# Splitting two neighbouring weight slabs with one instruction on each engine in a float32 two-layer trunk

## The chip, the cores and the metric

One Trainium2 chip, of which the kernel uses one core. The metric is the device time of one execution in microseconds (us); for the kernel before it is the median of three runs. The engines are TensorE (PE; its weight loads are listed as PEld), VectorE (DVE), ScalarE (ACT), GpSimd (POOL) and SyncE (SP). SP here only issues transfers.

## The reference, cut to what matters

The sequence has 256 tokens of width 2048, all in float32. Layer 0 mixes tokens with windowed attention, layer 1 with a gated block; each layer ends with an MLP of width 8192.

```python
for i in range(2):
    a = rms_norm(h, g[0])
    a = attention(a, w_qkv, w_o) if i == 0 else sgu_mixer(a, w_in, w_s, w_out)
    h = h + rms_norm(a, g[1])
    c = square(relu(rms_norm(h, g[2]) @ w_up[i])) @ w_down[i]
    h = h + rms_norm(c, g[3])
```

`sgu_mixer` takes `z = gelu(h @ w_in)`, splits it into u and v, normalises v over its width (mean and variance), mixes it over tokens with `w_s`, multiplies by u and projects with `w_out`.

## The kernel before, in words

**Products.** Every matrix product is made in three passes of TensorE: each float32 operand is split into a part `hi` that is rounded to the fp32r format and a rest `lo = raw - hi`, and hi*hi, hi*lo and lo*hi are summed (L396, L397, L398). The work is cut into 85 blocks. A block gives 256 tokens x 512 output columns from 2048 input rows, in 96 products of 128x512. Its weights come as eight slabs; a slab has two 128-row parts of 512 columns, 128x1024 in the on-chip memory, 512 KB. Slabs 2p and 2p+1 are pair p; PE takes pair by pair, and in each pair first token half 0 (both slabs), then token half 1. When the second half of a slab is done it counts `slab_used` up.

**Order of the blocks.** 0 is k and v, 1 to 4 are q, 5 to 8 the attention's output, 9 to 40 the first MLP, 41 to 44 the v half and 45 to 48 the u half of the gated block, 49 to 52 its output, 53 to 84 the second MLP. An MLP has four quarters of eight blocks: four up blocks, then four down blocks that add to y. The first quarter begins with `first_block`, in which the input is transposed while PE multiplies; the others begin with a plain block.

**A slab's way.** SP's `load_block` (L293 to L301) puts slab i into raw slot i mod 4 of `w_raw`; before it, it waits on `lo_made` until the slab four before has been subtracted. ACT's `split_slab` (L679 to L684) waits for the landing and until the slot i mod 8 of `w_hi` and `w_lo` is free (`slab_used`), and writes `w_hi`, rounded. DVE's `split_slab` (L1064 to L1067) waits for `hi_made`, writes `w_lo = w_raw - w_hi` and counts `lo_made` up by one, which gives the raw slot back to SP and the slab to PE. Both engines work three pairs (six slabs) ahead of PE: `slab_ahead(blk, i)` names slab i+6.

**Order on the engines.** It is written out by hand. `split_ahead(blk, pair)` calls `split_next` for the two slabs of a pair; `split_next` and the turns below take single slabs. In block 0 and in the attention's `attend` all slabs are single; around them, during the first q block (1), the calls on DVE are single slab 7 of block 0, pair 0, two small copies of v, pairs 1 and 2, single slab 6, the rotation of q (`rotate_q`, L1343 to L1348), and on ACT pairs 0 and 1, then a copy and a single slab twice. PE's next step, the transposes of q (L504), needs the rotation.

**Turns.** The result of up block j must be transposed to be the left operand of a down block. On ACT, the bank is drained (L811), then squared (L846); on DVE, `turn` (L1102 to L1109) makes four groups of four 32x32 transposes (L1098), each group followed by one single slab split; then ACT copies the result to `b_hi` (L710), DVE makes `b_lo` (L1114), and then both engines split pairs 2 and 3. Turn j runs on DVE during block j+1 of the quarter, the last in the first down block, whose pair 3 needs its `b_lo` (`first_down`). The order on ACT in such a block is pairs 0 and 1, `b_hi`, pairs 2 and 3, the drain of the block. In down blocks both engines split four pairs, then DVE adds the sum to y (L1201). In the second block of the first quarter both run behind `first_block`.

**The v half.** DVE takes statistics of each v block (L1491), averages them (L1516, L1519), and after one pair normalises (L1529, L1533) while PE is in block 45; PE's gate products (L653) come at four places in that block and wait for them.

Of the kernel before, what the change touches and what calls it, by code (L numbers as in the profile page):

```python
# [8 lines left out]
F32 = mybir.dt.float32  # L9
F32R = mybir.dt.float32r  # L10
I32 = mybir.dt.int32
ALU = mybir.AluOpType
ACT = mybir.ActivationFunctionType
# [11 lines left out]
RAW_SLOTS = 4  # L25
SLOTS = 8
LEAD = 3
PAIRS = KB // SLAB_KB // 2
# [24 lines left out]
BLOCKS = B_MLP1 + 2 * NB * QUARTERS  # L53
# [36 lines left out]
def trunk(nc, x, positions, gains, w_qkv, w_o, sinks, w_in, ln_g, ln_b, w_s, b_s, w_out, w_up, w_down, out):  # L90
    ctx = ExitStack()
    with ctx:
        def sb(name, shape, dt=F32):
            return ctx.enter_context(nc.sbuf_tensor(name, shape, dt))
# [4 lines left out]
        def sem(name):  # L99
            return ctx.enter_context(nc.semaphore(name))  # L100
# [8 lines left out]
        w_raw = sb("w_raw", [P, RAW_SLOTS, SLAB])  # L109
        w_hi = sb("w_hi", [P, SLOTS, SLAB], F32R)  # L110
        w_lo = sb("w_lo", [P, SLOTS, SLAB], F32R)
# [82 lines left out]
        slab_landed = [sem(f"slab_landed{i}") for i in range(RAW_SLOTS)]  # L194
# [5 lines left out]
        hi_made = sem("hi_made")  # L200
        lo_made = sem("lo_made")
        slab_used = sem("slab_used")
# [49 lines left out]
        def at_least(eng, sem_, value):  # L252

            if not isinstance(value, int) or value > 0:
                eng.wait_ge(sem_, value)
# [24 lines left out]
        def slab_ahead(blk, i):  # L280

            i = i + 2 * LEAD
            return (blk, i) if i < 2 * PAIRS else (blk + 1, i - 2 * PAIRS)
# [394 lines left out]
        def _(act):  # L678
            def split_slab(blk, i):  # L679

                act.wait_ge(slab_landed[i % RAW_SLOTS],
                            blk * (32 * PAIRS // RAW_SLOTS) + 16 * (i // RAW_SLOTS + 1))
                at_least(act, slab_used, blk * (2 * PAIRS) + (i + 1 - SLOTS))
                nc.scalar.activation(w_hi[:, i % SLOTS, :], w_raw[:, i % RAW_SLOTS, :], ACT.Copy).then_inc(hi_made, 1)  # L684
# [5 lines left out]
            def split_next(blk, *slabs):  # L690
                for i in slabs:
                    if not (isinstance(blk, int) and blk == BLOCKS - 1 and i + 2 * LEAD >= 2 * PAIRS):
                        split_slab(*slab_ahead(blk, i))

            def split_ahead(blk, pair):
                split_next(blk, 2 * pair, 2 * pair + 1)

            def split_unit(n, use0, norm, units=UNIT):

# [72 lines left out]
            def first_block(blk, use0, norm, evac):  # L772
# [9 lines left out]

                split_unit(2, use0, norm)
                split_ahead(blk - 1, 3)
                split_unit(3, use0, norm)
                split_unit(4, use0, norm)
# [12 lines left out]
                act.wait_ge(norm_done, norms[0])  # L799
                evac(0)  # L800
                split_ahead(blk, 2)
                evac(1)
                split_ahead(blk, 3)

            h_seen = [0]
# [253 lines left out]
        def _(dve):  # L1059
# [4 lines left out]
            def split_slab(blk, i):  # L1064

                dve.wait_ge(hi_made, blk * (2 * PAIRS) + (i + 1))
                nc.vector.tensor_tensor(w_lo[:, i % SLOTS, :], w_raw[:, i % RAW_SLOTS, :],  # L1067
                                        w_hi[:, i % SLOTS, :].bitcast(F32), ALU.subtract).then_inc(lo_made, 1)
# [5 lines left out]
            def split_next(blk, *slabs):  # L1074
                for i in slabs:
                    if not (isinstance(blk, int) and blk == BLOCKS - 1 and i + 2 * LEAD >= 2 * PAIRS):
                        split_slab(*slab_ahead(blk, i))

            def split_ahead(blk, pair):
                split_next(blk, 2 * pair, 2 * pair + 1)  # L1080

            def split_unit(n, use0, norm, units=UNIT):
                pair, t = units[n]
# [87 lines left out]
            def first_block(blk, use0, norm):  # L1171

                split_unit(2, use0, norm)
                split_ahead(blk - 1, 3)
                update_h(4)
                split_unit(3, use0, norm)
                update_h(5)
                split_unit(4, use0, norm)
                update_h(6)
                split_next(blk, 0)  # L1180
                split_unit(5, use0, norm)
                split_next(blk, 1)
                update_h(7)
                split_unit(6, use0, norm)
                split_next(blk, 2)
                split_unit(7, use0, norm)
                sums[0] += 2 * TOK
                dve.wait_ge(norm_sum, sums[0])
                link(nc.vector.tensor_tensor(sum_sq[:, :], pre_ssq[:, 0, :], pre_ssq[:, 1, :], ALU.add))
                mean()  # L1190
                inverse(r_in)
                split_next(blk, 3)
                split_ahead(blk, 2)
                split_ahead(blk, 3)
# [401 lines left out]
```

## Time and profile before

| what | value |
|---|---|
| median of three runs | 1921.07 us (1920.85 to 1921.43) |
| span of the profiled execution | 1919.6 us |
| PE busy | 1909.2 us, 99%, 8604 products and transposes |
| DVE busy | 1340.6 us, 70% |
| ACT busy | 959.1 us, 50% |
| bytes read from HBM | 365.52 MB, 192 GB/s over the span |
| granted clock of TensorE, mean | 0.999 |

The profiled execution's span goes from its first to its last instruction; what lies around it is in the run's time and not in the span, and the median of the runs is 1.5 us above this span. Times in rows are in us from the span's start; "mean ns" is the duration of one instruction. Two instructions one behind the other on ACT or DVE overlap by about 0.1 us, so that two of 1.06 take 2.0 together.

### The profile page before, as it was taken

To read this page: it belongs to the slowest core of one execution; us is meant where nothing else is said; L and a number is where in the kernel's file an instruction comes from. 1 tells how busy PE (TensorE), PEld (TensorE's weight loads), DVE (VectorE), ACT (ScalarE), POOL (GpSimd) and SP (SyncE) were. 2 spreads that over 40 slices of the span, in tenths; PEclk is the share of its full clock that TensorE was granted. 3 is DMA by queue.
4 is the path that set the end of the run, shared out by engine and by line. 5 is a ranking of instruction groups with operands and counts; after the bars stand their busy time and mean duration, and the time that the engine had idled before them with its cause. 6 is when DMAs were issued, how large, how long until landed. Compare 5 with 4: busy or idle time off the path is not lost.

```text
span 1919.6 us, 25731 instructions
## 1 busy us (share of the span) xinstructions
PE 1909.2 (99%) x8604; PEld 1572.2 (82%) x8604; DVE 1340.6 (70%) x1872; ACT 959.1 (50%) x1294; POOL 6.2 (0%) x23
## 2 busy tenths in 40 slices
PE   9999999999999999999999999999999999999998
PEld 7777888888888888888888888888888888888886
DVE  6886588657755865686768885787568557846864
ACT  7766475435534543544554454645354445434542
POOL 0000000000000000000000000000000000000000
PEclk9999999999999999999999999999999999999999
DMA  7546566655665565556485656566556655665663
GB/s 248 179 134 209 175 198 196 216 191 178 200 201 175 189 214 187 186 187 233 142 262 178 191 189 208 170 199 217 193 178 194 211 190 190 194 199 169 199 202 110
DMA packets 188691, 368.72 MB, mean 192 GB/s; under 512 B 11450, under 2 KB 11588, under 8 KB 187844
## 3 DMA queue, kind: packets, MB, share of 16 engines
q1 hardware_dynamic: 187280, 360.75, 58.2%
q0 software_dynamic: 1040, 6.82, 1.0%
q8 instruction: 51, 0.84, 0.2%
q14 instruction: 28, 0.23, 0.0%
q10 hardware_dynamic: 292, 0.08, 0.0%
HBM read 365.52 MB, written 2.10 MB: 192 GB/s over the span
## 4 chain that ended last, share of the span: by engine, by line
PE 98%; ACT 1%; DVE 1%; DMA 1%; issue 0%; SPq 0%; DVEq 0%; ACTq 0%
PE acc L396 16%; PE acc L398 16%; PE acc L397 16%; PE scores L396 15%; PE scores L398 15%; PE scores L397 15%; PE t L421 1%; PE scores L524 0%; PE o L543 0%; PE o L653 0%; DMA h<-in_x 0%; DMA w_raw<-in_attn_w_qkv 0%; DVE w_lo L1067 0%; PE t L534 0%; ACT L941 0%
## 5 line engine op out<-in xcount | busy, mean ns | idle before, releaser
L1067 DVE TENSOR_TENSOR w_lo<-w_raw,w_hi 128x1024 fp32r<-128x1024 f32 x679 | 818.9, 1223 | 314.7 <-ACT w_hi L684 297.7
L684 ACT ACTIVATE w_hi<-w_raw 128x1024 fp32r<-128x1024 f32 x679 | 703.7, 1057 | 529.9 <-PE scores L398 212.6
L1098 DVE STREAM_TRANSPOSE work<-s 32x256 f32<-32x256 f32 x544 | 237.1, 436 | 100.7 <-ACT s L846 90.8
L396 PE MATMUL acc<-w_hi,a_hi 128*128 128x512 f32 x768 | 303.4, 395 | 0.1
L398 PE MATMUL acc<-w_hi,a_lo 128*128 128x512 f32 x768 | 299.4, 390 | 0.0
L397 PE MATMUL acc<-w_lo,a_hi 128*128 128x512 f32 x768 | 299.0, 389 | 0.0
L396 PE MATMUL scores<-w_hi,a_hi 128*128 128x512 f32 x672 | 262.4, 390 | 0.0
L398 PE MATMUL scores<-w_hi,a_lo 128*128 128x512 f32 x672 | 261.5, 389 | 0.0
L397 PE MATMUL scores<-w_lo,a_hi 128*128 128x512 f32 x672 | 261.5, 389 | 0.0
L396 PE MATMUL acc<-w_hi,b_hi 128*128 128x512 f32 x640 | 249.8, 390 | 0.0
L396 PE MATMUL scores<-w_hi,b_hi 128*128 128x512 f32 x640 | 249.2, 389 | 0.0
L398 PE MATMUL acc<-w_hi,b_lo 128*128 128x512 f32 x640 | 249.1, 389 | 0.0
L397 PE MATMUL acc<-w_lo,b_hi 128*128 128x512 f32 x640 | 249.0, 389 | 0.0
L398 PE MATMUL scores<-w_hi,b_lo 128*128 128x512 f32 x640 | 249.0, 389 | 0.0
L397 PE MATMUL scores<-w_lo,b_hi 128*128 128x512 f32 x640 | 249.0, 389 | 0.0
L396 PEld LDWEIGHTS acc<-w_hi,a_hi 128*128 128x128 f32 x768 | 144.2, 188 | 31.5 <-issue 1.2
L398 PEld LDWEIGHTS acc<-w_hi,a_lo 128*128 128x128 f32 x768 | 144.2, 188 | 30.5
L397 PEld LDWEIGHTS acc<-w_lo,a_hi 128*128 128x128 f32 x768 | 144.3, 188 | 28.9
L396 PEld LDWEIGHTS scores<-w_hi,a_hi 128*128 128x128 f32 x672 | 126.2, 188 | 26.2 <-issue 0.2
L398 PEld LDWEIGHTS scores<-w_hi,a_lo 128*128 128x128 f32 x672 | 126.2, 188 | 26.2
L397 PEld LDWEIGHTS scores<-w_lo,a_hi 128*128 128x128 f32 x672 | 126.2, 188 | 25.9
L710 ACT ACTIVATE b_hi<-work 128x1024 fp32r<-128x1024 f32 x36 | 38.2, 1062 | 207.2 <-DVE work L1098 207.2
(159 smaller groups left out, 1396.6 us busy)
## 6 DMA issues: line engine op xcount, KB each, us to landing
w_raw<-in_mlp_w_up SPq DMA_DIRECT2D x256, 512.0 KB, 3.8
w_raw<-in_mlp_w_down SPq DMA_DIRECT2D x256, 512.0 KB, 4.6
w_raw<-in_sgu_w_in SPq DMA_DIRECT2D x64, 512.0 KB, 4.5
w_raw<-in_attn_w_qkv SPq DMA_DIRECT2D x39, 512.0 KB, 4.6
w_raw<-in_attn_w_o SPq DMA_DIRECT2D x32, 512.0 KB, 4.8
w_raw<-in_sgu_w_out SPq DMA_DIRECT2D x32, 512.0 KB, 4.6
gain<-in_norm_gains POOLq DMA_DIRECT2D x4, 1024.0 KB, 6.4
h<-in_x SPq DMA_DIRECT2D x8, 256.0 KB, 6.1
```

Source lines behind the costliest of these rows:

```text
L396: nc.tensor.matmul(bank[t][:, :], lhsT=x_hi[:, kb, tok], rhs=w1, start=(kb == 0), stop=False)
L397: nc.tensor.matmul(bank[t][:, :], lhsT=x_hi[:, kb, tok], rhs=w2, start=False, stop=False)
L398: last = nc.tensor.matmul(bank[t][:, :], lhsT=x_lo[:, kb, tok], rhs=w1, start=False, stop=(kb == KB - 1))
L421: last = nc.tensor.transpose(tb[n % 2][:, k * P:(k + 1) * P], h[:, t, f:f + P], ident[:, :])
L684: nc.scalar.activation(w_hi[:, i % SLOTS, :], w_raw[:, i % RAW_SLOTS, :], ACT.Copy).then_inc(hi_made, 1)
L710: nc.scalar.activation(b_hi[:, bass.ds(j * 4, 4), :], sT, ACT.Copy).then_inc(b_hi_made, 1)
L1067: nc.vector.tensor_tensor(w_lo[:, i % SLOTS, :], w_raw[:, i % RAW_SLOTS, :], w_hi[:, i % SLOTS, :].bitcast(F32), ALU.subtract).then_inc(lo ...
L1098: last = nc.vector.transpose(turned[:, :, :, src * 32:src * 32 + 32], part[:, :, :, dst * 32:dst * 32 + 32])
```

## The change

A pair that `split_ahead` asks for is now split by one instruction of 128x2048 on each engine, `split_two`. ACT waits for both slabs' landing and for the eight-slot buffer to have room for both, and counts `hi_made` up by two at the end; DVE waits for that, and counts `lo_made` up by two at the end. `split_next` and the four single splits of a turn stay as they were, and so do the loads of SP, each of which waits for its own slot.

```diff
--- before.py
+++ after.py
@@ -692,8 +692,18 @@
                     if not (isinstance(blk, int) and blk == BLOCKS - 1 and i + 2 * LEAD >= 2 * PAIRS):
                         split_slab(*slab_ahead(blk, i))
 
+            def split_two(blk, i):
+
+                for k in (i, i + 1):
+                    act.wait_ge(slab_landed[k % RAW_SLOTS],
+                                blk * (32 * PAIRS // RAW_SLOTS) + 16 * (k // RAW_SLOTS + 1))
+                at_least(act, slab_used, blk * (2 * PAIRS) + (i + 2 - SLOTS))
+                at, raw = i % SLOTS, i % RAW_SLOTS
+                nc.scalar.activation(w_hi[:, at:at + 2, :], w_raw[:, raw:raw + 2, :], ACT.Copy).then_inc(hi_made, 2)
+
             def split_ahead(blk, pair):
-                split_next(blk, 2 * pair, 2 * pair + 1)
+                if not (isinstance(blk, int) and blk == BLOCKS - 1 and 2 * pair + 2 * LEAD >= 2 * PAIRS):
+                    split_two(*slab_ahead(blk, 2 * pair))
 
             def split_unit(n, use0, norm, units=UNIT):
 
@@ -1076,8 +1086,16 @@
                     if not (isinstance(blk, int) and blk == BLOCKS - 1 and i + 2 * LEAD >= 2 * PAIRS):
                         split_slab(*slab_ahead(blk, i))
 
+            def split_two(blk, i):
+
+                dve.wait_ge(hi_made, blk * (2 * PAIRS) + (i + 2))
+                at, raw = i % SLOTS, i % RAW_SLOTS
+                nc.vector.tensor_tensor(w_lo[:, at:at + 2, :], w_raw[:, raw:raw + 2, :],
+                                        w_hi[:, at:at + 2, :].bitcast(F32), ALU.subtract).then_inc(lo_made, 2)
+
             def split_ahead(blk, pair):
-                split_next(blk, 2 * pair, 2 * pair + 1)
+                if not (isinstance(blk, int) and blk == BLOCKS - 1 and 2 * pair + 2 * LEAD >= 2 * PAIRS):
+                    split_two(*slab_ahead(blk, 2 * pair))
 
             def split_unit(n, use0, norm, units=UNIT):
                 pair, t = units[n]
```

## Rows read from the trace of the kernel before

**Rows 1.** the profile page: part 1's PE line and two groups of part 5
```profile
PE 1909.2 (99%) x8604; PEld 1572.2 (82%) x8604; DVE 1340.6 (70%) x1872; ACT 959.1 (50%) x1294; POOL 6.2 (0%) x23
...
L1067 DVE TENSOR_TENSOR w_lo<-w_raw,w_hi 128x1024 fp32r<-128x1024 f32 x679 | 818.9, 1223 | 314.7 <-ACT w_hi L684 297.7
L684 ACT ACTIVATE w_hi<-w_raw 128x1024 fp32r<-128x1024 f32 x679 | 703.7, 1057 | 529.9 <-PE scores L398 212.6
```

**Rows 2.** waits of the load queue: engine, line, releaser, us, times, longest
```profile
SPq L300 <- DVE w_lo L1067: 1415.0, 662, 14.5
```

**Rows 3.** instruction groups by form: the two half slabs of 512 columns
```profile
L1153 DVE TENSOR_TENSOR w_lo<-w_raw,w_hi 128x512 fp32r<-128x512 f32 x1 | 0.7, 686 | 0.0
...
L742 ACT ACTIVATE w_hi<-w_raw 128x512 fp32r<-128x512 f32 x1 | 0.6, 627 | 0.0
```

**Rows 4.** busy us (x count) of PE, PEld, DVE, ACT, POOL; clock, DMA, GB/s
```profile
300.00:322.00 22.00, 22.00 (x99) 18.23 (x98) 19.92 (x29) 11.40 (x13) 0.00 (x0) 1.00 0.66 212
```

**Rows 5.** DVE's timeline, start us and us, last pairs before the first turn
```profile
263.90 2.36 DVE L1067 TENSOR_TENSOR w_lo<-w_raw,w_hi 128x1024 fp32r<-128x1024 f32 x2 [1.50 <-ACT w_hi L684]
267.04 2.36 DVE L1067 TENSOR_TENSOR w_lo<-w_raw,w_hi 128x1024 fp32r<-128x1024 f32 x2 [0.78 <-ACT w_hi L684]
```

**Rows 6.** ACT's timeline in blocks 10 to 12
```profile
265.96 1.99 ACT L684 ACTIVATE w_hi<-w_raw 128x1024 fp32r<-128x1024 f32 x2
268.90 1.06 ACT L684 ACTIVATE w_hi<-w_raw 128x1024 fp32r<-128x1024 f32 x1 [0.95 <-DMA w_raw<-in_mlp_w_up]
270.99 1.06 ACT L684 ACTIVATE w_hi<-w_raw 128x1024 fp32r<-128x1024 f32 x1 [1.03 <-DMA w_raw<-in_mlp_w_up]
...
308.39 1.06 ACT L684 ACTIVATE w_hi<-w_raw 128x1024 fp32r<-128x1024 f32 x1 [1.18 <-DMA w_raw<-in_mlp_w_up]
```

**Rows 7.** DVE's timeline in blocks 11 to 13
```profile
303.30 1.23 DVE L1067 TENSOR_TENSOR w_lo<-w_raw,w_hi 128x1024 fp32r<-128x1024 f32 x1
...
312.08 1.77 DVE L1098 STREAM_TRANSPOSE work<-s 32x256 f32<-32x256 f32 x4 [1.36 <-ACT s L846]
...
331.83 1.78 DVE L1098 STREAM_TRANSPOSE work<-s 32x256 f32<-32x256 f32 x4 [1.25 <-ACT s L846]
...
343.95 1.22 DVE L1114 TENSOR_TENSOR b_lo<-work,b_hi 128x1024 fp32r<-128x1024 f32 x1
```

**Rows 8.** PE's timeline: first product of block 13, first of its fourth pair
```profile
329.31 0.39 PE L396 MATMUL acc<-w_hi,b_hi 128*128 128x512 f32 x1
...
345.63 0.39 PE L396 MATMUL acc<-w_hi,b_hi 128*128 128x512 f32 x1
```

**Rows 9.** start of the first head group: ACT's timeline, then the critical chain
```profile
47.81 1.06 ACT L684 ACTIVATE w_hi<-w_raw 128x1024 fp32r<-128x1024 f32 x1 [2.80 <-DMA w_raw<-in_attn_w_qkv]
...
54.20 1.23 DVE w_lo L1067
...
56.42 0.66 PE t L504 x4
```

**Rows 10.** the quarter of blocks 17 to 24: DVE's timeline, then PE's
```profile
517.21 1.22 DVE L1114 TENSOR_TENSOR b_lo<-work,b_hi 128x1024 fp32r<-128x1024 f32 x1
...
519.71 0.39 PE L396 MATMUL acc<-w_hi,b_hi 128*128 128x512 f32 x1
```

**Rows 11.** value blocks and layer norm: timelines of ACT, DVE and PE
```profile
969.04 1.06 ACT L684 ACTIVATE w_hi<-w_raw 128x1024 fp32r<-128x1024 f32 x1 [1.65 <-DMA w_raw<-in_sgu_w_in]
...
1024.96 1.06 ACT L684 ACTIVATE w_hi<-w_raw 128x1024 fp32r<-128x1024 f32 x1 [0.30 <-PE scores L398]
...
1032.21 0.17 DVE L1519 TENSOR_SCALAR mean_sq<-moments 128x2 f32<-128x2 f32 x1
...
1036.20 1.42 DVE L1533 SCALAR_TENSOR_TENSOR y<-y,r_out,work 128x512 f32<-128x512 f32 x2
...
1038.30 0.38 PE L653 MATMUL o<-y,work 128*128 128x256 f32 x1
```

**Rows 12.** loads issued from 985.0 to 986.6 us: time to landing
```profile
DMA to landing us min/median/max: 7.3/7.3/7.3
```

## The prediction

> **What bounds the kernel now.** I read the page first. TensorE (PE) is busy 1909.2 of 1919.6 us [rows 1], so only about 10 us are idle, nearly all before the first product. An edit that takes no product away can gain next to nothing in the middle; it can only lose, where it makes PE wait. VectorE (DVE) and ScalarE (ACT) are at 70% and 50%: idle there costs nothing by itself. The same rows show the two instructions that are merged, 679 of each: 1057 ns on ACT, 1223 ns on DVE, DVE waiting mostly for ACT and ACT mostly for PE.
>
> Next the load queue's own waits: SP waits 1415 us for the DVE subtraction that gives a raw slot back [rows 2]. So the loads run as early as the four raw slots allow, and a slot's round trip (given back, loaded, rounded by ACT, subtracted by DVE) is what to watch. Then the timeline where DVE is fullest: it is busy 19.92 of 22 us in the second to fourth block of the first MLP [rows 4]. Nine times (eight quarters and the gated block's output) such a chain of turns ends in a down product, and there I compared DVE's end with PE's need.
>
> **PE's pace.** Block 13 (the first down block of MLP 0) starts at 329.31 and its fourth pair at 345.63 [rows 8]: 5.44 us a pair, 21.76 us a block. Four raw slots are one turn of 10.88 us.
>
> **Costs of the parts.** *ACT:* 128x512 takes 626 ns, 128x1024 takes 1057 [rows 1, 3]: 431 ns per 512 columns, so 128x2048 takes about 1.91 us, against 1.99 for two back to back. Ends 1.91 (slope) and 2.1 (two full ones); I take 1.91. *DVE:* 686 and 1223 ns [rows 1, 3] give 2.30 us, against 2.36 for two [rows 5]; ends 2.30 and 2.45. So merging saves some 0.1 us of engine time a pair, in idle engines, worth nothing to PE. *The new waits:* ACT waits for both landings and for the second slab's split slots (PE ends it six products, 1.36 us, after the first slab's); DVE waits for both w_hi; both raw slots come free at the end of 2.30 us. Behind ACT's wait stand its drains of PE's banks, behind DVE's the transposes, the rotation and the norm.
>
> *One slot's trip:* a subtraction ends at 303.30+1.23=304.53 and ACT starts on the slab loaded into that slot at 308.39 [rows 6, 7]: 3.9 us with the issue. *Two slots at once:* no row shows it. The nearest: two slots given back 1.14 us apart, at 265.12 and 266.26 (the two end at 263.90+2.36 [rows 5], the first 1.14 sooner), and ACT starts on their successors at 268.90 and 270.99 [rows 6]. The second came 4.7 us after its own slot, 5.9 after the first's. So a pair takes between 4.7 and 5.9; I take 5.3, the middle, because the two transfers clearly share something and start now together.
>
> The Trainium skill, "SBUF — State Buffer", The DMA setup-cost knee, fits a DMA as about 2 us plus bytes at 436 GB/s; by it a pair of 1 MiB would be 4.4 us, an estimate from that page, and the sum below would be near 11 us instead of 18.
>
> Plain blocks: 5.3+1.91+2.30+0.1=9.6 us against 10.88. They keep pace; a merged slab is ready 16.32-1.91-2.30=12.1 us ahead of PE, a single one 14.0. Cost zero, covered by the three pairs of lead. What follows are the four places with no such cover.
>
> **1. First query block, about +2.9 us.** Here PE waits already: its transposes at 56.42 come after DVE's rotation of q (L1343 to L1348), which stands behind the single subtraction of 54.20 to 55.43 [rows 9], that behind ACT's rounding, and that behind a load into the first slot of what is now a merged pair. That pair's second slab reaches ACT only at 47.81 [rows 9]. Merged: ACT 47.8 to 49.7, DVE to 52.05, both slots back; +3.9 gives ACT 55.95 to 57.0, DVE to 58.25. The rotation starts 58.25-55.43 = 2.8 us later, and so does PE, with small change 2.85. Ends 2.7 and 3.9 (load 3.7 to 4.9).
>
> **2. and 3. First quarter of each MLP, +6.1 us each.** The turn in DVE is four groups of transposes (1.78) and four single subtractions (1.23), 12.1 us. After it the last slot's load (3.9), ACT's rounding, ACT's drain of the finished block (from 308.39+1.06=309.45 to the next transposes at 312.08: 2.63 [rows 6, 7]) and the next turn. Before: 12.1+3.9+1.06+2.63=19.7, as 312.08 to 331.83 is [rows 7]. That is 2 us a block less than PE, so DVE catches up, and its last b_lo ends at 343.95+1.22=345.17 for a need at 345.63: 0.5 us of room.
> After, by steps. The pair before the first turn ends its subtraction at about 270.6 instead of 267.04+2.36=269.40 [rows 5] (ACT can start between 265.96 [rows 6] and 266.9, where its second single one did; the middle). First transposes at 270.6. The first single subtraction of the turn waits for a merged w_hi: slots back at 267.0, +5.3, +1.91 = 274.2, 1.85 us of wait. Turn over at 284.65; +3.9+1.91 = 290.45; drains 2.6, b_hi 1.05, b_lo 1.22: second turn at 295.4. Its successor: 12.1+3.9+1.91+2.6 = 20.5, at 315.9; the next again with 1.05 of wait for the merged w_hi, at 337.45. b_lo of the fourth turn ends 1.0+12.1+1.22 later, 351.8. PE needs it at 345.63: +6.1. DVE no longer catches up, because the period is 21.6. At 4.7 for a pair it is 4.3, at 5.9 it is 7.9. The second MLP has the same order and offsets; I count it alike.
> The other six quarters, and the chain before block 49, begin from a plain block: there the last b_lo ends at 517.21+1.22=518.43 for a need at 519.71 [rows 10], and the turns start when PE ends, not behind the loads: by the same steps they stay 0.1 to 0.3 late, under 1.28. Cost zero; gone, if a pair takes over 6.5.
>
> **4. Value blocks and layer norm, +3.0 us.** The first merged pair starts on ACT at 969.04 with its load late [rows 11]; DVE done 973.3. Six trips of 9.6 and about 1.5 of contention with the gate weights' load (two slabs issued there took 7.3 us to land [rows 12], some 1.5 over a pair's 5.9) end at 1032.4; at PE's pace they would end at 1029.2 (ACT free to start at 1024.96 [rows 11], +1.91+2.30), in time for the statistics. Then transposes 0.9, statistics 1.4, means 0.4: mean_sq at 1035.2 instead of 1032.21. The normalised half ends at 1036.20+1.42 and PE's gate wants it at 1038.30 [rows 11]: 0.7 of room, so PE waits 2.3; the fourth gate, behind two more merged subtractions, 0.7 more. Ends 0.9 (pair 4.7) and 6.
>
> **Sum.** 2.85+6.1+6.1+3.0 = 18.0 us on a profiled 1919.6 us span; the median of the runs, 1921.07, is 1.5 above the span, and I add to it: **1939.1 us**. Ends: 2.7+8.6+0.9=12.2, and 3.9+15.8+6=25.7.
>
> **Rivals.**
> *A, the forecast* (waits at four places), chance 0.70.
> *B, loads of a pair land nearly together,* ACT served after 4.2 us. For: issues will be 0.4 us apart, not 1.14. Against: 268.90 and 270.99, 2.1 apart. By the same steps a quarter costs 2.9, the norm 0.5, place 1 the same: 1921.07+9.2=1930.3, a little less if more than that is covered. Chance 0.12.
> *C, not slower:* with fewer loads in flight each is served sooner, in place 2 above all, where the last slot's load stands in every turn. The point from which it decides is 3.0 us for one load (in place of 3.9) and 3.8 for two: then each quarter loses 0.8, place 1 2.0, the norm nothing, 3.6 in all: 1924.7, and 1922 if it is faster still. For: between two pairs the queue is now empty for longer. Against: in a turn slots come back 3.05 us apart, so those loads were nearly alone already and took the 3.9. Chance 0.08.
> *D, all blocks:* if a pair's trip passes 6.6 us, the round exceeds 10.88 everywhere; at 7.0 it is 0.8 us a block, some 50 us over about 70 blocks less the lead: about 1960. For: two loads took 7.3 us beside another [rows 12]. Against: that was one place, and the round has 1.3 us to spare. Chance 0.08.
> *E, faster:* in 300 to 322 DVE is nearly full [rows 4]; two merged subtractions save 0.12 a block, 0.5 in a quarter. That gives 1920.6, with the short wait before 56.42 gone. It is faster by over 0.2% only if much else shifts. Chance 0.02.
> The Trainium skill, "Perfetto Trace Analysis", Optimizing Scalar/DVE Operations, says both: grouping helps a saturated engine (E), and where the engine is not saturated but causes bubbles elsewhere, breaking instructions up may finish work sooner. By the second this change is the wrong way round; with DVE at 70% of the span the trace bears out the second.
>
> **Range and chances.** Ends of A are 1933 and 1947; downwards I take in most of B: 1928 to 1947, leaving out C, D and E. A measurement of this kernel tells about 0.2%, 3.8 us. Faster 0.02, same 0.08 (C), slower 0.90 (A, B, D).
>
> **What would show it.** In the changed trace: subtractions of 2.30 and roundings of 1.91; slabs of a pair reaching ACT 5.3 after the subtraction; the first q transposes near 59.3; a PE gap of about 6 us at the fourth pair of blocks 13 and 57 with b_lo as its end, none in the other six; a gap of about 2 us at the first gate. PE's other steps 0.227 us as before. Wrong would be: PE busy share still 99% of a span under 1924, or waits for w_lo in the plain blocks (D).

## The result, and the profile after

The changed kernel takes 1954.91 us (median of five runs, 1953.37 to 1957.82) against 1921.09 (1920.85 to 1921.43, five runs): a ratio of 1.0179, 95% interval 1.0168 to 1.0189. It is slower, as forecast, but by 33.8 us and not by 18.0, and the time lies outside the range of 1928 to 1947. The profiled execution has a span of 1951.6 us, the shortest of its five (the others 1952.6 to 1956.0), and 1.8 us lie around it; before it was 1919.6. The 32.0 us between these two spans are what is accounted for below.

The page of the changed kernel, to be read beside [rows 1]:

```profile
PE 1916.3 (98%) x8604; PEld 1576.3 (81%) x8604; DVE 1317.0 (67%) x1634; ACT 911.1 (47%) x985; POOL 6.2 (0%) x23
...
L702 ACT ACTIVATE w_hi<-w_raw 128x2048 fp32r<-128x2048 f32 x309 | 591.6, 1915 | 695.2 <-DMA w_raw<-in_mlp_w_down 210.3
L1093 DVE TENSOR_TENSOR w_lo<-w_raw,w_hi 128x2048 fp32r<-128x2048 f32 x238 | 545.6, 2292 | 488.2 <-ACT w_hi L702 486.7
```

The instructions last what was forecast: 1.915 us on ACT, 2.292 on DVE. Both engines work less, ACT by 48 us and DVE by 24. PE executes the same 8604 instructions and is nevertheless busy for 7.1 us longer: besides waiting, it ran slower somewhere, which the table below finds. Next, PE's waits in the changed kernel (what waited, the releaser: us in total, times, longest):

```profile
PE acc L396 <- DVE b_lo L1132: 15.7, 2, 8.2
PE t L504 <- DVE s L1366: 2.8, 1, 2.8
PE acc L396 <- DVE w_lo L1093: 2.8, 3, 0.9
PE o L653 <- DVE y L1551: 2.4, 1, 2.4
...
PE o L653 <- DVE y L1559: 1.0, 1, 1.0
```

Four of these lines belong to the four forecast places: the last `b_lo` of the two first quarters (one line), the rotated q, and the two lines of the norm. The `w_lo` line was not forecast.

To divide the 32.0 us, the start of each product was compared with the start of the same product before; each row is a step in the difference.

| where | step, us | forecast |
|---|---|---|
| the start of the kernel | -0.8 | 0 |
| q transposes before block 2 | +2.7 | 2.85 |
| the next products of block 2 | +1.5 | 0 |
| blocks 9, 41, 53, fifth slab | +1.2 each, 3.5 in all | 0 |
| block 13, fourth pair | +8.3 | 6.1 |
| the rest of block 13 | +2.4 | 0 |
| block 45, gate; block 46 | +2.65 and +1.2 | 2.3 and 0.7 |
| block 49 | +0.3 | 0 |
| block 57, fourth pair | +7.7 | 6.1 |
| the rest of block 57 | +2.5 | 0 |

The third, sixth and last rows are places where PE waits for nothing and still falls behind. The windows of the changed kernel behind the wait in block 13 show why (columns as in [rows 4]; the clock stands before the DMA share):

```profile
350.00:358.00 8.00, 0.36 (x2) 0.00 (x0) 7.42 (x12) 3.81 (x3) 0.00 (x0) 0.69 0.51 166
358.00:362.00 4.00, 3.49 (x8) 2.81 (x9) 2.75 (x2) 1.46 (x2) 0.00 (x0) 0.50 0.43 131
362.00:366.00 4.00, 4.00 (x16) 3.18 (x15) 2.50 (x2) 1.40 (x1) 0.00 (x0) 0.84 0.78 255
366.00:370.00 4.00, 4.00 (x20) 3.30 (x19) 1.97 (x3) 1.92 (x1) 0.00 (x0) 1.00 0.74 217
```

PE stands idle from 350.4 to 358.5, and while it stands its granted clock falls from 1.0 to 0.5, from 2.4 to 1.2 GHz. The products after the wait find it there. PE's timeline of the changed kernel, at the same place:

```profile
358.51 0.79 PE L396 MATMUL acc<-w_hi,b_hi 128*128 128x512 f32 x1 [8.15 <-DVE b_lo L1132]
359.10 0.63 PE L397 MATMUL acc<-w_lo,b_hi 128*128 128x512 f32 x1
359.53 0.63 PE L398 MATMUL acc<-w_hi,b_lo 128*128 128x512 f32 x1
359.95 0.63 PE L396 MATMUL acc<-w_hi,b_hi 128*128 128x512 f32 x1
```

The steps are 0.43 us instead of 0.227. The clock is at half from 353.1 to 363.3, from 1342.9 to 1353.1 and from 59.5 to 62.9. In block 2 it fell only at 59.5, 1.2 us after PE had started again at 58.35.

### The profile page after: what moved, and what is told of

It reads as the page before. It is cut to its first block, busy times and chain, and to the rows that moved or that the text cites. A ratio compares the mean times of both kernels' runs of the same rounds, so it can differ in the third digit from the quotient of the medians.

```text
span 1951.6 us, 25457 instructions
## 1 busy us (share of the span) xinstructions
PE 1916.3 (98%) x8604; PEld 1576.3 (81%) x8604; DVE 1317.0 (67%) x1634; ACT 911.1 (47%) x985; POOL 6.2 (0%) x23
## 4 chain that ended last, share of the span: by engine, by line
PE 86%; DVE 6%; ACT 3%; DMA 3%; issue 2%; SPq 0%; ACTq 0%; DVEq 0%
PE acc L396 14%; PE acc L397 14%; PE acc L398 14%; PE scores L396 14%; PE scores L398 14%; PE scores L397 14%; ACT w_hi L702 2%; DVE work L1116 2%; DVE w_lo L1093 2%; DMA w_raw<-in_mlp_w_up 2%; DVE w_lo L1077 1%; DMA w_raw<-in_mlp_w_down 1%; PE t L421 1%; PE scores L524 0%; PE o L543 0%
## 5 line engine op out<-in xcount | busy, mean ns | idle before, releaser
L702 ACT ACTIVATE w_hi<-w_raw 128x2048 fp32r<-128x2048 f32 x309 | 591.6, 1915 | 695.2 <-DMA w_raw<-in_mlp_w_down 210.3
L1093 DVE TENSOR_TENSOR w_lo<-w_raw,w_hi 128x2048 fp32r<-128x2048 f32 x238 | 545.6, 2292 | 488.2 <-ACT w_hi L702 486.7
L1077 DVE TENSOR_TENSOR w_lo<-w_raw,w_hi 128x1024 fp32r<-128x1024 f32 x203 | 247.3, 1224 | 24.4 <-ACT w_hi L702 16.6
L396 PEld LDWEIGHTS acc<-w_hi,b_hi 128*128 128x128 f32 x640 | 121.3, 190 | 43.3 <-DVE b_lo L1132 16.9
```

Source lines behind the costliest of these rows:

```text
L396: nc.tensor.matmul(bank[t][:, :], lhsT=x_hi[:, kb, tok], rhs=w1, start=(kb == 0), stop=False)
L702: nc.scalar.activation(w_hi[:, at:at + 2, :], w_raw[:, raw:raw + 2, :], ACT.Copy).then_inc(hi_made, 2)
L1093: nc.vector.tensor_tensor(w_lo[:, at:at + 2, :], w_raw[:, raw:raw + 2, :], w_hi[:, at:at + 2, :].bitcast(F32), ALU.subtract).then_inc(lo_m ...
```

## The experiments

Each variant is told by its difference from the kernel before or from the changed one. Where only one time is given, one run was timed beside the kernel before (1920.8 to 1921.2 us) and its span and steps are what is compared, with 1919.6. The five spans of the changed kernel lie 4.4 us apart, so where two variants that wait like it differ by less in their totals, only the steps at the places tell something.

### Which engine's half costs what

The first run merges on ACT alone, the second on DVE alone, each with the other engine's `split_ahead` as before:

```diff
 def split_ahead(blk, pair):        # of the engine that stays as before
-    if not (isinstance(blk, int) and blk == BLOCKS - 1 and 2 * pair + 2 * LEAD >= 2 * PAIRS):
-        split_two(*slab_ahead(blk, 2 * pair))
+    split_next(blk, 2 * pair, 2 * pair + 1)
```

> ACT rounds a pair with one instruction, DVE subtracts slab by slab and gives each raw slot back by itself. Theory T (the joint give-back lengthens a raw slot's trip): the waits shrink but stay, since the rounding still waits for both landings and ends 0.9 us later than the second single one: about 0.5 us at the first q transposes, 0.3 at each of the three first blocks, 4 to 6 with some clock loss at each first quarter, 1 to 2 at the norm; the span is 12 to 18 us over the 1919.6 of before. Rival R (DVE's instruction of 128x2048, which cannot start before both w_hi and blocks its engine for 2.3 us, is the cause): with it gone the span is within 3 us of before.

> ACT rounds slab by slab as before, DVE subtracts a pair with one instruction and gives both slots back together. Theory T: about 2 us at the first q transposes, 1.2 at each of the three first blocks (the pair's w_lo is late for PE's fifth slab), 0.6 at block 13 and nothing at block 57, because the turns' period stays at 19.8 us and DVE catches up, 1.5 to 2.5 at the norm; the span is 6 to 10 us over before. Rival R (the DVE instruction is the cause of all): over 20 us.

ACT alone: 1939.98 us, span +18.6, which is 0.6 over its range. DVE alone: 1929.04 us, span +7.6, inside its range, but in part by luck: the norm costs 0.3 us in all where 1.5 to 2.5 were expected, block 13 nothing where 0.6 was, and 1.6 us went behind q at half clock, which was not in the sum. PE's waits with ACT alone merged:

```profile
PE acc L396 <- DVE b_lo L1131: 10.2, 2, 5.5
PE t L504 <- DVE s L1365: 1.7, 1, 1.7
```

And with DVE alone merged:

```profile
PE acc L396 <- DVE w_lo L1092: 3.1, 3, 1.0
PE t L504 <- DVE s L1365: 2.0, 1, 2.0
```

So the two halves hurt at different places. ACT's merge makes the last `b_lo` late in both first quarters; DVE's alone never does, but it makes the three first blocks lose 1.3 us each. Together they cost 32.0, which is 5.8 more than 18.6 and 7.6. By places, the waits of the two first quarters grow from 10.5 us (ACT alone) and nothing (DVE alone) to 16.0, and the gate in block 45, which neither alone delays, loses 2.65; at q and in the first blocks the two together cost less than the sum. In the quarters and at the gate one delay feeds the other.

### The waits without the long instructions

Two more variants of the kernel before, all slabs still split one by one. In the first, DVE counts `lo_made` up by two at a pair's second subtraction, so both slots come back together; in the second, ACT waits for both landings before the first rounding.

```diff
-                split_next(blk, 2 * pair, 2 * pair + 1)
...
+                for half in range(2):
+                    b, i = slab_ahead(blk, 2 * pair + half)
+                    dve.wait_ge(hi_made, b * (2 * PAIRS) + (i + 1))
+                    last = nc.vector.tensor_tensor(w_lo[:, i % SLOTS, :], w_raw[:, i % RAW_SLOTS, :],
+                                                   w_hi[:, i % SLOTS, :].bitcast(F32), ALU.subtract)
+                last.then_inc(lo_made, 2)
```

> The kernel before with one edit on DVE: a pair's two subtractions stay single but count lo_made up only after the second, by two. Theory T: nearly as the kernel in which DVE alone is merged, 5 to 9 us over before, since the slots and the slabs come free at the same times within 0.1 us; if the instruction's size is what costs, under 2 us.

```diff
+                b, i = slab_ahead(blk, 2 * pair)
+                act.wait_ge(slab_landed[(i + 1) % RAW_SLOTS],
+                            b * (32 * PAIRS // RAW_SLOTS) + 16 * ((i + 1) // RAW_SLOTS + 1))
                 split_next(blk, 2 * pair, 2 * pair + 1)
```

> The kernel before with one edit on ACT: before the first of a pair's two roundings it waits for both landings; all instructions are single. Theory T: slots come back 1.1 us apart, so the second lands some 4.7 us after its own and the first rounding waits for it; 0.5 us or less at the q transposes, 0 to 2 at block 13, the norm under 1: the span is 1 to 5 us over before. If the wait alone explains ACT's share, it comes near the kernel in which ACT alone is merged (12 us or more).

The joint give-back alone: 1924.10 us, span +2.7, below what was expected. Of it 0.7 are at the q transposes and 0.8 at each of blocks 9, 41 and 53; nothing at 13 or 57. The joint wait alone: 1925.45 us, span +4.1, as expected, of which 2.3 stand at block 13 and 1.65 at block 57. PE's waits, with the joint give-back and then with the joint wait:

```profile
PE acc L396 <- DVE w_lo L1085: 1.5, 3, 0.5
```

```profile
PE acc L396 <- DVE b_lo L1119: 3.6, 2, 2.1
```

Each is small. Are the long instructions the rest? This run takes the changed kernel and writes each merged instruction as two of 128x1024, while all its waits and counts stay joint:

```diff
-    nc.scalar.activation(w_hi[:, at:at + 2, :], w_raw[:, raw:raw + 2, :], ACT.Copy).then_inc(hi_made, 2)
+    nc.scalar.activation(w_hi[:, at, :], w_raw[:, raw, :], ACT.Copy)
+    nc.scalar.activation(w_hi[:, at + 1, :], w_raw[:, raw + 1, :], ACT.Copy).then_inc(hi_made, 2)
...                                    # likewise for the subtraction on DVE
```

> The changed kernel with each merged instruction written again as two of 128x1024, while every wait and every count stays joint (ACT waits for both landings and both split slots, counts two at the end; DVE waits for both w_hi, gives both slots back at the end). If the loss comes from the joint waits and the joint give-back, the span stays within 3 us of the changed kernel's 1951.6, with the long waits at the fourth pair of blocks 13 and 57. If the long instructions themselves cost it, or if the separate effects simply add (4.1 of waiting for both landings and 2.7 of the joint give-back), the span is 1925 to 1931.

1957.09 us, span 1955.3: 3.7 above the changed kernel's and so 0.7 outside the 3 us, but nowhere near 1931. Most of the 3.7 is the norm, where the step is 5.8 us and 3.4 us at half clock fell. The page of this variant shows the instructions apart again, and its waits the same stall:

```profile
L702 ACT ACTIVATE w_hi<-w_raw 128x1024 fp32r<-128x1024 f32 x309 | 326.9, 1058 | 665.4 <-DMA w_raw<-in_mlp_w_down 203.1
...
L703 ACT ACTIVATE w_hi<-w_raw 128x1024 fp32r<-128x1024 f32 x309 | 322.2, 1043 | 0.0
```

```profile
PE acc L396 <- DVE b_lo L1135: 15.8, 3, 7.9
PE o L653 <- DVE y L1554: 3.9, 1, 3.9
```

The length of the instruction is therefore not the cause. What costs is that a pair is handed on only when it is complete, at three places in a row: landing to ACT, ACT to DVE, DVE to the slots. The handoff from ACT to DVE is in this run and in neither of the two small ones. No run has it alone, so its share is argued and not shown: between the joint wait (+4.1) and ACT merged (+18.6) lie 14.5 us, 4.4 of them at half clock, and what differs is this handoff, ACT's wait for both slabs' room in `w_hi`, and the one instruction.

### Where the loss stands

The changed kernel with single slabs in the first quarter of each MLP alone; its complement, merged pairs there and single slabs elsewhere, has the two values of the flag exchanged:

```diff
             def split_ahead(blk, pair):
+                if one[0]:
+                    split_next(blk, 2 * pair, 2 * pair + 1)
-                if not (isinstance(blk, int) and blk == BLOCKS - 1 and 2 * pair + 2 * LEAD >= 2 * PAIRS):
+                elif not (isinstance(blk, int) and blk == BLOCKS - 1 and 2 * pair + 2 * LEAD >= 2 * PAIRS):
...
+                one[0] = True
                 quarter(0, base, True, False)
+                one[0] = False
```

> The changed kernel with single slabs on both engines in the first quarter of each MLP (blocks 9 to 16 and 53 to 60), pairs elsewhere. If the quarters' waits and the slow clock after them are all of that place's loss: 32.0 less 8.3+2.4 and 7.7+2.5 and two first-block waits of 1.15 leaves about 9 us over before (span near 1928.5). If the pairs cost everywhere and the waits only show it there, it stays over 20 us.

> The kernel before with merged pairs in the first quarter of each MLP alone, the complement of the run with single slabs there. By the places: two waits of about 8 us, two stretches at half clock behind them of 2.4, and the first blocks 9 and 53 at 1.2 each: 23 us, a span near 1942.8. If the 4.5 us that the changed kernel has already lost by then is part of why the quarters are so dear, it is under 1938.

Single there: 1932.00 us (1930.85 to 1935.44, four runs), ratio 1.0060 (1.0045 to 1.0076), span +10.9. That span is 2 us above the 9 expected: PE loses 0.9 us at block 49 and 1.3 on the way into block 53, where the changed kernel lost 0.3 and nothing. Merged there alone: 1943.09 us (1940.84 to 1943.33, four runs), ratio 1.0116 (1.0099 to 1.0133), span +19.5. The two losses add up to 1.76% beside 1.79% for the whole change. PE's waits in the second:

```profile
PE acc L396 <- DVE b_lo L1142: 14.4, 2, 7.5
```

There block 13 waits 7.6 us and block 57 7.1, though PE came to block 13 only 0.6 us late and not 4.6: being late on entry is not what makes the quarters dear. Its span is 3.7 us below the sum that was expected, since the waits are shorter by 1.3 us together and the clock is at half for 6.8 us behind each instead of 10.2.

### The half clock

The changed kernel with 30 extra products on PE, whose result nobody reads, just ahead of the fourth pair of blocks 13 and 57:

```diff
             def first_down(blk, index, idle=0):
                 for pair in range(PAIRS):
+                    if pair == PAIRS - 1:
+                        idle_products(idle)
```

> The changed kernel with 30 extra products into an unused bank (6.8 us at full clock) ahead of the wait at the fourth pair of blocks 13 and 57; their result is never read. Clock theory: TensorE's granted clock fell to 0.5 after the two long waits and cost 2.4 us at each; with PE at work in the wait it stays at 1.0, and the span is 4.5 to 5 us under the changed kernel's 1951.6. Rival (the slow steps are the restart's own, or the products delay the kernel): the same or up to 3 us more.

Windows of this variant, behind the wait and then at the norm:

```profile
358.00:362.00 4.00, 4.00 (x19) 3.28 (x18) 2.29 (x1) 0.89 (x2) 0.00 (x0) 1.00 0.56 132
362.00:366.00 4.00, 4.00 (x20) 3.30 (x19) 2.73 (x2) 1.17 (x1) 0.00 (x0) 1.00 0.71 252
...
1052.00:1060.00 8.00, 5.24 (x17) 4.27 (x18) 7.89 (x11) 1.61 (x1) 0.00 (x0) 0.79 0.51 170
```

The clock stays at 1.00 behind both quarters. The fourth pair starts 7.9 us late in each, as before, and there is no step behind it: the 2.4 and 2.5 us of the table were the clock's. The span is 1949.2, only 2.4 under the changed kernel's where about twice that was expected, because this time 3.4 us at half clock fell into the norm, where the step grew from 2.65 to 4.75, block 49 lost 1.1 us instead of 0.3, and 0.7 us less was gained at the start of the kernel; on the other side, the 1.5 us at half clock behind q didn't come. The median of its runs is 1952.98 us (1950.98 to 1956.75, four runs), ratio 1.0172 (1.0157 to 1.0188), not separable from the changed kernel's.

### What bounds a turn

In the first quarter the chain to `b_lo` runs through three turns. The starts of the four `b_lo` of the first quarter give their period, here the mean of the last two:

| kernel | the four `b_lo` start at | period |
|---|---|---|
| before | 290.77, 304.57, 324.33, 343.95 | 19.7 |
| joint give-back, singles | 292.04, 305.86, 325.35, 344.96 | 19.6 |
| DVE merged | 295.65, 309.46, 329.06, 348.83 | 19.7 |
| joint landing wait, singles | 291.29, 305.10, 325.86, 346.47 | 20.7 |
| ACT merged | 294.74, 308.55, 330.42, 351.80 | 21.6 |
| all joint, in two instructions | 299.03, 312.84, 335.30, 357.31 | 22.2 |
| changed | 298.69, 312.50, 334.89, 357.24 | 22.4 |

A block on PE takes 21.76 us [rows 8], so at 19.7 DVE gains on PE and at 22.4 it loses. The forecast had ACT's drain of the finished block behind the last merged rounding and ahead of the next transposes. The next run puts the drain before that rounding, in the first quarters only:

```diff
                         split_ahead(blk + j, 2)
-                        split_ahead(blk + j, 3)
                         up_evac(blk + j, j)
+                        split_ahead(blk + j, 3)
```

> The changed kernel, in the first quarter of each MLP with ACT's drain and squaring of a finished up block moved ahead of the rounding of the fourth pair. Theory T (the turn's start stands behind the last slot's load and the merged rounding): the chain loses 3.9+1.9 us a turn where PE's block is long done, so the turns catch up and the 8 us waits at blocks 13 and 57 shrink to under 3, without a slow clock; the span is 14 to 21 us under the changed kernel's 1951.6. Rival (the pair's own trip sets the turns): under 5 us is gained.

1952.91 us, span 1951.1: 0.5 us less than the changed kernel's. The two waits fall only by 0.9 and 1.3 us, some of it given back at other steps, and the period is still 22.4. The theory that the drain carries the loss falls. In the changed kernel the end of a turn and the start of the next are, on DVE,

```profile
314.20 2.29 DVE L1093 TENSOR_TENSOR w_lo<-w_raw,w_hi 128x2048 fp32r<-128x2048 f32 x1 [0.47 <-ACT w_hi L702]
318.28 2.29 DVE L1093 TENSOR_TENSOR w_lo<-w_raw,w_hi 128x2048 fp32r<-128x2048 f32 x1 [1.79 <-ACT w_hi L702]
320.80 1.77 DVE L1116 STREAM_TRANSPOSE work<-s 32x256 f32<-32x256 f32 x4 [0.23 <-ACT s L856]
324.44 1.23 DVE L1077 TENSOR_TENSOR w_lo<-w_raw,w_hi 128x1024 fp32r<-128x1024 f32 x1 [1.86 <-ACT w_hi L702]
```

and on ACT

```profile
316.26 1.92 ACT L702 ACTIVATE w_hi<-w_raw 128x2048 fp32r<-128x2048 f32 x1 [2.16 <-DMA w_raw<-in_mlp_w_up]
318.08 0.67 ACT L821 ACTIVATE s<-acc,r_in 128x512 f32<-128x512 f32 x1
...
320.02 0.63 ACT L856 ACTIVATE s<-s 128x512 f32<-128x512 f32 x1
322.49 1.92 ACT L702 ACTIVATE w_hi<-w_raw 128x2048 fp32r<-128x2048 f32 x1 [1.83 <-DMA w_raw<-in_mlp_w_up]
```

The drain ends at 320.65, DVE's own merged subtraction at 320.57. The two are side by side, and taking away one leaves the other. With the drain moved, DVE's timeline reads

```profile
317.90 2.29 DVE L1098 TENSOR_TENSOR w_lo<-w_raw,w_hi 128x2048 fp32r<-128x2048 f32 x1 [1.99 <-ACT w_hi L702]
320.11 1.77 DVE L1121 STREAM_TRANSPOSE work<-s 32x256 f32<-32x256 f32 x4
324.29 1.23 DVE L1082 TENSOR_TENSOR w_lo<-w_raw,w_hi 128x1024 fp32r<-128x1024 f32 x1 [2.41 <-ACT w_hi L702]
```

The transposes start 0.7 us sooner, and the first single subtraction waits 0.55 longer for the same merged rounding. What bounds the changed kernel here is the trip of the pair that DVE gave back at 314.20+2.29=316.49, which ACT starts at 322.49. So the next theory was the merged rounding in the turn. In the first quarters ACT takes the turn's four slabs one by one, DVE stays as changed; then the same with the drain moved as well:

```diff
-                        split_ahead(blk + j, 0)
-                        split_ahead(blk + j, 1)
+                        split_next(blk + j, 0, 1, 2, 3)    # first quarters only; likewise for blk + NB
```

> The changed kernel, but in the first quarter of each MLP ACT rounds the four slabs of a turn (pairs 0 and 1) one by one, as VectorE subtracts them there in any case; all else stays merged. Theory: the trip from VectorE's joint give-back of pairs 2 and 3 to ACT's merged rounding of the next turn's slabs bounds the turns, and 0.9 us of each is the long rounding and about 1 us the wait for the second landing; then the period of a turn falls back to about 19.7 us, the waits at the fourth pair of blocks 13 and 57 fall from 8 us to under 2, the half-clock stretch behind them goes, and the span is 1932 to 1937. Rival: the joint give-back on VectorE bounds it; then the waits stay over 5 us and the span over 1944.

> As the kernel before this one in the list (single roundings for the turn's slabs), and ACT's drain moved ahead of the fourth pair's rounding in these blocks. If the drain is late next once the merged rounding is gone, a further 1 to 2 us; if it never is, the same within 0.5 us, as when it was moved alone.

Single roundings: 1947.15 us, span 1945.2, waits of 4.6 and 5.1 us; period 20.6. That is neither theory whole: the span is over 1944, as the rival has it, one wait is under its 5 us and one just over, and neither is under 2. The wait at the turn's first subtraction did go, as DVE's timeline of this run shows:

```profile
318.22 2.29 DVE L1099 TENSOR_TENSOR w_lo<-w_raw,w_hi 128x2048 fp32r<-128x2048 f32 x1 [1.71 <-ACT w_hi L702]
320.74 1.78 DVE L1122 STREAM_TRANSPOSE work<-s 32x256 f32<-32x256 f32 x4 [0.22 <-ACT s L856]
322.53 1.23 DVE L1083 TENSOR_TENSOR w_lo<-w_raw,w_hi 128x1024 fp32r<-128x1024 f32 x1
```

It was 1.86 us of the period of 22.4. The other 0.9 over before is in the first two rows: the turn's last slot is loaded last, lands at 316.05, and then the pair takes ACT 1.92 and DVE 2.29, to 320.51; a slab by itself would take 1.06+1.23=2.3 instead of 4.5, and before it was the drain that ended last. With the drain moved as well: 1940.79 us, span 1938.9, 6.3 us less where 1 to 2 were expected. The waits in the quarters fall to 3.1 and 3.6; 3.0 of the 6.3 come from them, and most of the rest from stretches at half clock behind q and block 13 that this run doesn't have. So the drain does matter once the merged rounding is gone, by 1.5 us a quarter, 1.2 of it ahead of the first `b_lo` already (296.39 against 298.70, with 1.1 us less lost on entry).

### Pairs only where the lead covers them

Merged pairs in blocks 17 to 40 and 61 to 84 alone, single slabs elsewhere:

```diff
+            one = [True]               # on both engines; False once the first quarter is over
...
+            one[0] = True              # ahead of the v half's first_block
             first_block(B_V, T_V, 4)
```

> Pairs only where three pairs of lead cover them (blocks 17 to 40 and 61 to 84), single slabs everywhere else. Theory T: the place decides, not the instruction; no wait is left, the span is within 1 us of 1919.6 and the time the same as before within 0.1%. If merged instructions cost PE anything by themselves (through shared memory or queues), it is slower in proportion, 5 us or more.

1921.48 us (1920.77 to 1923.02, eleven runs) against 1921.00 (fifteen runs), ratio 1.0004 (0.9995 to 1.0013). The page of this variant:

```profile
PE 1908.8 (99%) x8604; PEld 1572.0 (82%) x8604; DVE 1327.3 (69%) x1732; ACT 929.2 (48%) x1106; POOL 6.3 (0%) x23
...
L702 ACT ACTIVATE w_hi<-w_raw 128x2048 fp32r<-128x2048 f32 x188 | 359.9, 1915 | 413.9 <-DMA w_raw<-in_mlp_w_down 171.3
...
L1100 DVE TENSOR_TENSOR w_lo<-w_raw,w_hi 128x2048 fp32r<-128x2048 f32 x140 | 321.0, 2293 | 294.9 <-ACT w_hi L702 294.9
```

188 of ACT's 309 pairs and 140 of DVE's 238 are merged, ACT and DVE are busy for 30 and 13 us less, and nothing is won. No version ran that beats the kernel before.

## Why the prediction was right and wrong

**The sign and four of the places were right.** PE had no slack to win, the cost appears as PE's waits, and the releasers are those named: `b_lo` in blocks 13 and 57, the rotation, the norm. The other six quarters and the plain blocks lose nothing, as said, and block 49 0.3 us; in the v half ACT takes every second pair after 9.8 us (1020.45 to 1030.29), under the 10.88 of four slabs on PE, so rival D is out. For the six quarters the run with pairs only there confirms it with an interval. Rivals B (4.2 us to ACT) and C (3.8) are out too: the shortest trip in the trace is 5.3.

**Place 1 was sized right, its sequel was not foreseen.** The transposes of q start at 58.35, with a wait of 2.8 us and a step of 2.7 against 2.85 forecast (they were forecast near 59.3; the rest is the 0.8 us that the start of the kernel gained), but then 1.5 us go in products at half clock. The step that failed is "PE's other steps 0.227 us as before": what a wait does to the clock behind it was put at nothing. With 2.4 and 2.5 behind blocks 13 and 57 this is 6.4 us, the largest part of the 14.0 missing.

**Places 2 and 3: the mechanism right, the size not.** 8.3 and 7.7 us against 6.1, 3.8 in all. In block 13 the forecast steps hold within 0.35 us up to the third turn once the 4.55 us lost earlier are added (transposes at 300.24 against 295.4, at 320.80 against 315.9). The third turn then lasts 22.6 us against 21.55, and from the fourth to the end of `b_lo` it is 15.0 against 14.3. The mis-sized term is the wait for the merged `w_hi`, 1.05 and 1.0 in the forecast and 1.86 and 1.30+0.41 in the trace, and in it the trip of two slots. It was taken as 5.3 us from give-back to ACT; here it is 322.49-316.49=6.0, and 5.65 a turn later; from 1012 to 1042 us, in the v half, it is 5.3 to 5.7. Over the 112 merged roundings of the trace that waited for a load into two slots given back together it is 5.3 to 7.8, with a median of 5.7, so 5.3 was the shortest and not the middle. The forecast's own far end, 5.9 for a pair, gave 7.9 us a quarter, near the 8.3 and 7.7 measured. The last 0.41 comes from a pair whose two loads took 6.1 and 6.8 us to land, where the loads issued from 316 to 343 us took 3.7 to 5.1:

```profile
346.50 1.23 DVE L1077 TENSOR_TENSOR w_lo<-w_raw,w_hi 128x1024 fp32r<-128x1024 f32 x1 [1.30 <-ACT w_hi L702]
...
353.01 1.23 DVE L1077 TENSOR_TENSOR w_lo<-w_raw,w_hi 128x1024 fp32r<-128x1024 f32 x1 [0.41 <-ACT w_hi L702]
```

I also put the drain alone on the path, where DVE's subtraction of the last pair ends with it; that didn't change the sum, but it made me expect a remedy from moving the drain that didn't come.

The Trainium skill, "SBUF — State Buffer", The DMA setup-cost knee, would have made the pair 4.4 us, taken as one transfer of 1 MiB, an estimate from its fit. The trace does not agree. Between 1010 and 1050 us the second load, half of those bytes, lands 4.4 to 4.8 us after its own issue; SP issues it 0.6 us after the first, so the pair takes 5.0 to 5.5 from the first issue, and 0.16 from the give-back to that issue comes on top. The measurement decides: 5.3 to 7.8, with the median of 5.7.

**Place 4 was nearly right:** 2.65 and 1.2 us against 2.3 and 0.7. The square's mean ended 3.9 us late against 3.0. DVE's and PE's timelines of the changed kernel:

```profile
1052.48 0.17 DVE L1537 TENSOR_SCALAR mean_sq<-moments 128x2 f32<-128x2 f32 x1
...
1056.41 1.42 DVE L1551 SCALAR_TENSOR_TENSOR y<-y,r_out,work 128x512 f32<-128x512 f32 x2
```

```profile
1057.31 1.97 PE L653 MATMUL o<-y,work 128*128 128x256 f32 x8 [2.38 <-DVE y L1551]
```

**The three first blocks were missed, 3.5 us.** The step that failed is "What follows are the four places with no such cover": the first blocks had been put among the covered ones. In `first_block` PE goes through slabs 0 to 5 for token half 0 before it turns to half 1, so it asks for slab 4 sooner than the count of three pairs of lead says. Before, that slab was ready 0.4 us ahead (its subtraction ended at 245.14; PE wanted it at about 245.55). In the changed kernel it is half of a pair of 2.29 us:

```profile
247.81 2.29 DVE L1093 TENSOR_TENSOR w_lo<-w_raw,w_hi 128x2048 fp32r<-128x2048 f32 x1 [0.39 <-ACT w_hi L702]
```

```profile
250.25 0.47 PE L396 MATMUL acc<-w_hi,a_hi 128*128 128x512 f32 x1 [0.92 <-DVE w_lo L1093]
```

The give-back run shows it in its purest form: 0.8 us there from the later count alone, since slab 4 is counted only with slab 5.

**The sum.** 6.4 (half clock) + 3.5 (first blocks) + 3.8 (quarters) + 0.9 (norm) + 0.3 (block 49) - 0.1 (q) - 0.8 (start) = 14.0, which is 32.0 less 18.0. The medians differ by 1.8 us more than the two spans; the runs now differ by 4.5 us among themselves, 0.6 before. It is not shown that the half clock makes this spread: the mean granted clock was 0.993 both in the fastest run (1953.37 us) and in the slowest (1957.82).

What the Trainium skill says in "Perfetto Trace Analysis", Optimizing Scalar/DVE Operations, on engines that are not saturated but cause bubbles, is the half of its advice that held here: both engines got cheaper, and PE waited. It is the handoffs that must be broken up, though: the instructions broken up alone, with all waits and counts joint, gave nothing back (span 1955.3).

**Open:** what makes the pair's trip vary from 5.3 to 7.8 us; how much eight raw slots would give back, which no run tried; the share of the handoff from ACT to DVE alone; why the start of the kernel gains 0.1 to 0.8 us in the variants; and why the clock falls behind some waits and not behind others.

## What to carry to other kernels

Merging two producer steps joins three handoffs as well: the wait for both inputs, the signal to the next engine, and the return of both buffers. Price those; the saved instruction overhead is nothing on an engine that is not the bound. The two halves apart cost 18.6 and 7.6 us and together 32.0, so test the whole ring of buffers, and not only each link.

Lead in a pipeline is measured to the first consumer in its own order. A place that takes the slabs in another order (here the first block) has less lead than the rest, and is found by comparing each buffer's ready time with its need, not by counting stages.

Where PE has been made to wait for some microseconds, reckon a second price for the products that follow at half clock: here 1.4 to 2.9 us a time, and nothing behind several of the waits up to 3.2 us.

## What was not expected of the hardware

The granted clock fell to half in or just behind some waits of PE and not others of the same length. At q, 3.4 us were at half clock behind a wait of 2.0 us (DVE merged) and of 2.8 (changed kernel), and none behind 2.8 in the last of the turn runs and behind 3.2 in the run with single slabs in the first quarters; that run had none behind 2.8 at the norm either. In the last turn run the wait at block 13 cost 3.1 us and was followed by no half clock, the one at block 57 cost 3.6 and was followed by 6.8 us of it. Behind 4.6 to 5.7 it was 6.8 or 3.4 us, behind 6.4 to 8.3 it was 10.2 or 6.8. Each such stretch cost 1.4 to 2.9 us. PE's steps in them were 0.427 us in place of 0.227.

DVE's subtraction of 128x2048 starts 0.10 us after the end of the rounding that it waits for (318.18 to 318.28, 314.10 to 314.20), and one of 128x1024 0.03 after it (48.87 to 48.90 in the kernel before, from the rounding of 47.81 [rows 9]). It goes with DVE's instruction and not with ACT's: where ACT alone is merged it is 0.03 behind roundings of 128x2048, and where DVE alone is merged 0.10 behind roundings of 128x1024, in nearly all of over 200 cases each.
